# Unused words between SBUF tensors: where row buffers start relative to the split weights, modulo 512 bytes

## The reference, cut to what matters

```python
x = x + moba_attention(hn, ...)                                # layer 0 of the first network
x = x + sq_relu_mlp(rms_norm(x, ln_mlp[i]), mlp_w_up[i], mlp_w_down[i])   # both layers, width 4096
x = x + dsa_attention(hn, ...)                                 # layer 1
...
h = h + rwkv/s5 mixer;  h = h + memory_cross_attention(...)    # second network, layer 0
h = h + swiglu(hn, ff_w_gate, ff_w_up, ff_w_down)              # width 2816
h = h + diff_attention(...);  h = h + memory_cross_attention(...)
h = h + moe_swiglu(hn, ...)                                    # 8 experts, top 2, width 3584
```

## The kernel before, in words

| tensor | remainder before | remainder after | off `weights_split` before | after |
|---|---|---|---|---|
| `weights_split` | 288 | 160 | - | - |
| `normed_split` | 160 | 160 | -128 | 0 |
| `rows_split`, first MLP | 288 | 224 | 0 | +64 |
| `rows_split`, second MLP | 288 | 416 | 0 | +256 |
| `rows_split`, third (gated) MLP | 288 | 288 | 0 | +128 |
| `rows_split` of cross attention, `source_split` | 288 | 160 | 0 | 0 |
| `XG` | 288 | 224 | 0 | +64 |
| `HT` | 288 | 288 | 0 | +128 |
| `ring` | 128 | 128 | -160 | -32 |

## Time and profile before

### The profile page before, as it was taken

The page is one execution under the profiler, slowest core; times in us unless marked ns, Lnnn a source line. Parts: engine busy times, 40 slices in busy tenths (PEclk is TensorE's granted clock), DMA queues, the critical chain, the costliest instruction groups (busy, mean ns, idle before and its releaser), DMA issues. The chain is left out here.

```text
span 2724.6 us, 37245 instructions
## 1 busy us (share of the span) xinstructions
PE 2533.9 (93%) x13514; PEld 2073.2 (76%) x13515; DVE 1887.8 (69%) x2297; ACT 1501.0 (55%) x1845; POOL 208.5 (8%) x226
## 2 busy tenths in 40 slices
PE   7899887998968899998979989999999999999998
PEld 6688775786846587887758768887887888888887
DVE  4565536666558675666567579985555989898898
ACT  3544434444321254544455468884445888888886
POOL 0000002295033100000100000000000000000000
PEclk9999979999977799999989989999999999999999
DMA  9355431556110443555424459995555999999995
GB/s 309 108 187 188 154 98 61 172 181 203 42 43 2 155 155 124 170 186 170 141 76 155 132 195 367 348 374 180 185 185 181 366 347 376 337 378 345 366 351 219
DMA packets 305176, 566.14 MB, mean 208 GB/s; under 512 B 22073, under 2 KB 126856, under 8 KB 304680
## 3 DMA queue, kind: packets, MB, share of 16 engines
q1 hardware_dynamic: 305064, 564.59, 60.1%
HBM read 561.19 MB, written 6.50 MB: 208 GB/s over the span
## 5 line engine op out<-in xcount | busy, mean ns | idle before, releaser
L1744 DVE TENSOR_TENSOR weights_split<-ring,weights_split 128x1024 fp32r<-128x1024 f32 x676 | 814.8, 1223 | 214.2 <-ACT weights_split L1739 186.4
L1887 PE MATMUL ps<-weights_split,expert_split 128*128 128x512 f32 x3864 | 900.5, 392 | 5.4 <-DVE weights_split L1744 2.6
L1739 ACT ACTIVATE weights_split<-ring 128x1024 fp32r<-128x1024 f32 x676 | 715.8, 1062 | 294.8 <-PE ps L1887 294.8
L1887 PEld LDWEIGHTS ps<-weights_split,expert_split 128*128 128x128 f32 x3864 | 723.4, 189 | 157.5 <-DVE weights_split L1744 4.8
L293 DVE TENSOR_TENSOR weights_split<-ring,weights_split 128x2048 fp32r<-128x2048 f32 x182 | 417.8, 2296 | 338.4 <-ACT weights_split L284 334.9
L284 ACT ACTIVATE weights_split<-ring 128x2048 fp32r<-128x2048 f32 x182 | 344.9, 1895 | 321.4 <-PE ps L464 152.8
L369 PE MATMUL ps<-weights_split,normed_split 128*128 128x512 f32 (+1 forms) x1944 | 464.8, 396 | 22.2 <-DVE normed_split L823 7.7
L369 PEld LDWEIGHTS ps<-weights_split,normed_split 128*128 128x128 f32 x1944 | 363.0, 192 | 109.0 <-issue 17.8
L463 PE MATMUL ps<-rows_split,weights_split 128*128 128x512 f32 x992 | 353.9, 399 | 1.4 <-DVE rows_split L507 1.1
L464 PE MATMUL ps<-rows_split,weights_split 128*128 128x256 f32 x992 | 278.0, 280 | 0.0
L463 PEld LDWEIGHTS ps<-rows_split,weights_split 128*128 128x128 f32 x992 | 186.3, 188 | 49.9 <-DVE rows_split L507 2.7
(11 more groups left out here) (456 smaller groups left out, 2232.3 us busy)
## 6 DMA issues: line engine op xcount, KB each, us to landing
ring<-moe_w_gate SPq DMA_DIRECT2D x112, 1024.0 KB, 5.5
ring<-moe_w_up SPq DMA_DIRECT2D x112, 1024.0 KB, 5.5
ring<-moe_w_down SPq DMA_DIRECT2D x112, 1024.0 KB, 5.1
ring<-mlp_w_up SPq DMA_DIRECT2D x32, 1024.0 KB, 5.4
ring<-mlp_w_down SPq DMA_DIRECT2D x32, 1024.0 KB, 4.9
ring<-xa_w_kv SPq DMA_DIRECT2D x16, 1024.0 KB, 5.2
ring<-moba_w_qkv SPq DMA_DIRECT2D x12, 1024.0 KB, 11.6
ring<-da_w_qkv SPq DMA_DIRECT2D x12, 1024.0 KB, 5.1
```

The lines of the kernel that those rows point to most:

```text
L1739: nc.scalar.activation(split_piece(p, 0), ring_piece(p), ACT.Copy).then_inc(high.sem, 1)
L1744: nc.vector.tensor_tensor(split_piece(p, 1), ring_piece(p), split_piece(p, 0).bitcast(F32), ALU.subtract)\
L1887: last = nc.tensor.matmul(ps[:, banks[part if down else half][tt], :], stationary(s, k, tt), split_piece(p, i)[:, part * NW:(part + 1) * N ...
```

## The change

Unused words are put between tensors. 96 words behind `normed_split` move everything that is allocated later by 384 bytes. 16, 64 and 32 words ahead of the three MLPs' `rows_split`, and 16 words ahead of each of the experts' two buffers, which become two allocations. No instruction is added, removed, or moved: on all five engines the rows of the program are the same in the same order, only addresses differ.

```diff
         self.XS = nc.alloc_sbuf_tensor("normed_split", [P, 2, KD, T], F32R)
+        sb("gap", [P, 96])
         self.kept_constants = const_at["onehot"][0]
...
-def project_mlp(core, gain_col, n, gated=False, beside=None, sp=None):
+def project_mlp(core, gain_col, n, gated=False, beside=None, sp=None, space=0):
+    space_guard = core.scoped("space", [P, max(space, 1)])
+    if space:
+        space_guard.__enter__()
     guard = core.scoped("rows_split", [P, 2, KD, T], F32R)
...
-    guard = core.scoped("expert_split", [P, 2, 2, D], F32R)
-    split_room = guard.__enter__()
-    XG, HT = split_room[:, 0], split_room[:, 1]
+    space = core.scoped("space", [P, 16])
+    space.__enter__()
+    guard = core.scoped("gathered_split", [P, 2, D], F32R)
+    XG = guard.__enter__()
+    hidden_space = core.scoped("space", [P, 16])
+    hidden_space.__enter__()
+    hidden_guard = core.scoped("hidden_split", [P, 2, D], F32R)
+    HT = hidden_guard.__enter__()
...
-    project_mlp(core, at_col("ln_mlp"), DFF // NF, sp=load_late)
+    project_mlp(core, at_col("ln_mlp"), DFF // NF, sp=load_late, space=16)
...
-    project_mlp(core, at_col("ln_mlp", 8), DFF // NF, beside=mixer, sp=sp)
+    project_mlp(core, at_col("ln_mlp", 8), DFF // NF, beside=mixer, sp=sp, space=64)
...
-    project_mlp(core, at_col("norm_ffn_2"), FF2 // NF, gated=True)
+    project_mlp(core, at_col("norm_ffn_2"), FF2 // NF, gated=True, space=32)
```

More of the change, by code:

```diff
@@ L680, in project_mlp @@
     guard.__exit__(None, None, None)
+    if space:
+        space_guard.__exit__(None, None, None)
 class Mlp:
@@ L2222, in mixture @@
     rows_guard.__exit__(None, None, None)
+    hidden_guard.__exit__(None, None, None)
+    hidden_space.__exit__(None, None, None)
     guard.__exit__(None, None, None)
+    space.__exit__(None, None, None)
 def rwkv_s5(core, w, l0, col, at_col, small, ws_guard, mixer):
```

## The result

The changed kernel takes 2736.6 us (median of 7 runs, 2730.5 to 2746.9) against 2722.6 for the kernel before in runs beside it: ratio 1.0043, 95% interval 1.003 to 1.0056, so 8 to 15 us slower. The profiled execution took 2740.09 us with a span of 2738.3, 13.7 us more than before. The forecast was faster by 14.

The account below looks back on a forecast made before the run. TensorE's matmul pace was taken as the bound; -15.6 + 0 + 1.5 + 0 = -14.1 us brought the profiled 2724.6 to 2710.5, forecast as a 2708 us median, range 2686 to 2734.

Parts of the forecast that it names:

- The cause: TensorE's matmul pace follows the stationary buffer's distance to the weights: 6.2 ns between two buffers in the dense expert.
- Step 1: Products from `normed_split`, moved from -128 to 0, get faster: -15.6 us, bounds -13 to -20.
- The wide form's 5 ns a pair: Pairs of 512 and 256 columns from `normed_split`: 5 of 9 ns credited to distance, 1.9 us over 384 pairs.
- Step 2: Slot experts' 2352 matmuls from `XG`, moved from 0 to +64: taken as 0, between 32.0 us less and 14.6 more.
- Step 3: Experts' 1512 matmuls from `HT`, moved from 0 to +128: taken as +1.5 us, between -20.6 and +9.4.
- the row at -128: `normed_split`'s slower pace in the dense expert, 6.2 ns a matmul, taken as near but not the same as +128.
- Step 4: The three MLPs' `rows_split` moved to +64, +256 and +128: taken as 0, bounds -28 and +7.8 us.
- Step 5: Everything else, such as ScalarE's and VectorE's copies at shifted distances: taken as 0, hidden by 1.30 us slack a round.
- Any distance from 0 costs, on either side: Rival, chance 0.29: moved expert and MLP buffers slow by +20.4 us, net +4.8, 2727 us; 2734 if `XG` pays 6.2 ns.
- point of decision: Mean loss of 4.0 ns a matmul over `XG` and `HT`, from which the change would be slower than before.
- The cap of 46 us: Most that `XG` and `HT` products could gain in slots rounds, 49 by 72 by 13.1 ns; below VectorE's limit of 64.
- The positive side is the good one: Rival, chance 0.24: cost falls from -128 over 0 to +128, so experts and MLPs gain; total -35, 2687 us.

Follow-up runs that it names:

- e1: The changed kernel with only the spaces ahead of the experts' `XG` and `HT` undone, both back at distance 0: 2716.5 us, ratio 0.9973 to the kernel before.
- e7: The kernel before plus only the experts' spaces (`XG` at +64, `HT` at +128), no gap, MLP rows at 0: 2750.7 us, ratio 1.0087.
- e9: Every row buffer at distance 0, except low half of `XG` 64 bytes off and low half of `HT` 256 off: 2721.6 us in one execution.
- e2: The kernel before plus only the gap behind `normed_split`, so every row buffer stands at distance 0: 2716.3 us, ratio 0.9967.

## Why the prediction was wrong

- *The bound* was read rightly: TensorE's pace sets the time, and nothing took over when it became slower. A round grew by 0.39 us, all of it between starts of matmuls.
- *The cause* was read rightly too: it is the distance to the weights that counts, not the own remainder (e1, e7), which had 0.85. That the load and the stream get in each other's way is not shown (e9).
- *Step 1, `normed_split` to 0,* had the right pace and too large a sum. The dense products gained 5.4 ns each by the measure above (6.2 taken), line 369's 4.7 at full clock (232.4 to 227.7). But 15.6 us were booked, and the profiled execution shows 3.8 up to the experts and 2.5 in the dense one; e2, where nothing else changes, gives 6 to 12 us by its interval. Part of what is missing lies in stretches in which TensorE waits for split weights: the second MLP's waits went from 3.1 to 4.0 us, and the third MLP's down products and wide stretches together gained nothing. "TensorE is the bound in all these stretches, so it is taken in full" was the weak sentence. The wide form's 5 ns a pair were half a misreading of a stretch that ends in a handover: with gaps of 450 ns and more left out, the 384 pairs from `normed_split` went from 352.6 to 349.9 ns, 2.7 each and 1.0 us in all. The MLPs' pairs do not even share the sign: there +384, which is -128, is 2.4 ns cheaper than 0.
- *Step 2, `XG` to +64, is the step that failed.* It was taken at 0, and costs 233.4 - 227.5 = 5.9 ns by 2352 = 13.9 us. The bound above, 14.6, held it. The reason given, that the only witness of a loss stands twice as far away, assumed that cost grows with distance. It does not: 32 bytes cost as much as 128.
- *Step 3, `HT` to +128,* was taken at +1.5, and costs 5.1 by 1512 = 7.7 us; both steps together are 21.6 where 19.4 were seen start to start, as part of it goes under in waits: the distances of 300 ns and more, which the paces leave out, sum to 31.4 us before and 23.4 after. +128 and -128 are the same place on a circle of 256 bytes, so the row at -128 was not a mirror but the thing itself, and its 6.2 ns should have been taken whole. Steps 2 and 3 together were 17.9 us off (19.4 for 1.5) and step 1 was 9.3 off (6.3 for 15.6): 27.2 of the 27.8 us between the forecast for the profiled execution, 2710.5, and its span of 2738.3.
- *Step 4, the MLPs:* near nothing, as taken. The first gains 3.6 ns a pair (352.8 to 349.2), 0.9 us, the second nothing at +256, and the third, at +128, alternates between some 351 and 358 a pair and gained nothing either.
- *Step 5:* VectorE's copies stayed at 1222 ns, ScalarE's at 1065 (1223 and 1062 before).
- *The rivals.* "Any distance from 0 costs, on either side" is what happened at +64 and +128 in the token form; its terms for the MLPs, 3.7 us in all, did not come. Its point of decision, 4.0 ns in the mean over both buffers, was passed: 5.6. Its price with the full 6.2 for `XG`, 2734 us, is close to the 2736.6 measured; with step 1 at its true size it would have been 2740 or more. The cap of 46 us on the gains was worked out with 13.1 ns a matmul where the excess is 13.6 (48 us); it played no part. "The positive side is the good one" rested on the 13.6 ns of excess alone, and got 0.24. The range ended at 2734, 2.6 us short.
- *The rule of the Trainium skill* in "TensorE: Matmul & The Clock Gate", Part 2, that loading the next weights takes no read bandwidth from the running matmul, was taken to mean that no distance matters. That conclusion does not hold for these float32r products: between two placements of the same buffer lie 5.9 ns of 233, and e7 prices both buffers' places at 0.7 to 1.0% of the kernel. Whether read bandwidth is what is lost no run here shows.

## What to carry to other kernels

Where matmuls of a long run follow each other at their own pace, look at the distance of two starts by operand buffer: two groups of one shape with different paces can be a sign of placement, and the pace at the better one is what the other can have. A price for a new place is not to be interpolated between two known ones: look for a period first, and move one buffer at a time, since here one edit held a gain of 0.3% and a loss of 0.9%. A gain in pace is worth its full sum only where no wait stands close behind; the waits for the next operand have to be read stretch by stretch.

## What the runs showed of the hardware

For float32r matmuls of 512 columns with a stationary load of 128 columns each, the pace is 226.8 to 227.9 ns when the stationary operand starts a multiple of 256 bytes from the moving one, or 16 bytes below that (tried once), and 229 to 234.5 at the other distances tried, save +16, where stretches run at either 227 or 233. A start 4 bytes off, which is also off any multiple of 16, had 232.6. For pairs of 512 and 256 columns with the weights stationary the pace is 347.2 to 360.4 a pair ns, and the best distances are others (+16, +32, +160). The granted clock is 1.00 in the windows shown, and distances at the half clock (426 ns) are left out. Why the circle has 256 bytes, why 192 and 240 are low, and what picks the pace at +16, no run here tells.
